# One decoder layer on one core: probabilities times values as unsplit fp32, two heads in two column groups

## What is computed

```python
probs = jax.nn.softmax(jnp.where(mask, q @ k.T * SCALE + bias, -jnp.inf), axis=-1)
y_head = probs @ v                                   # own
y_head = g0 * (p_cmp @ v_cmp) + g1 * (p_slc @ v_slc) + g2 * (p_win @ v_win)   # NSA, gates g
x = x + (sig(gA) * (y_A @ W_A) + sig(gB) * (y_B @ W_B)) @ W_o
x = x + (gelu(conv_a) * conv_b) @ W_down             # conv of rms_norm(x) @ W_up
x = x + sig(x @ W_pg) * (p @ W_pp)
```

## Time and profile before

| | us |
|---|---|
| median of 3 runs (lowest, highest) | 928.82 (927.83, 929.5) |
| the profiled execution | 928.06 |
| its span | 926.0 |
| TensorE busy | 888.6 (96%) |
| VectorE, ScalarE, GpSimd busy | 426.5, 411.1, 434.7 |
| attention steps, roughly | 88 to 410 |

### The profile page before, as it was taken

The page is one execution under the profiler, slowest core; times in us unless marked ns, Lnnn a source line. Parts: engine busy times, 40 slices in busy tenths (PEclk is TensorE's granted clock), DMA queues, the critical chain, the costliest instruction groups (busy, mean ns, idle before and its releaser), DMA issues.

```text
span 926.0 us, 13400 instructions
## 1 busy us (share of the span) xinstructions
PE 888.6 (96%) x4601; PEld 766.5 (83%) x4601; DVE 426.5 (46%) x961; ACT 411.1 (44%) x893; POOL 434.7 (47%) x557
## 2 busy tenths in 40 slices
PE   8999899998999799999999999999999999999998
PEld 8898798897899678787788788888888888888886
DVE  5445756866756545545412644444444440021124
ACT  5224554654746354644344454444444442232321
POOL 4841653554533433655363374444444445454350
PEclk9999999999999899999999999999999999999999
DMA  6835323333121034436543453333333333332213
GB/s 205 183 97 151 101 67 95 89 68 95 46 58 47 14 91 133 139 127 228 183 143 91 137 160 93 101 93 101 91 92 96 98 97 108 101 92 91 91 58 136
DMA packets 101365, 99.33 MB, mean 107 GB/s; under 512 B 15956, under 2 KB 76084, under 8 KB 101300
## 3 DMA queue, kind: packets, MB, share of 16 engines
q1 hardware_dynamic: 101247, 98.48, 36.4%
q10 hardware_dynamic: 53, 0.01, 0.0%
HBM read 87.58 MB, written 10.88 MB: 106 GB/s over the span
## 4 chain that ended last, share of the span: by engine, by line
PE 82%; DVE 7%; POOL 3%; ACT 3%; issue 3%; DMA 1%; SPq 0%; ACTq 0%; DVEq 0%; POOLq 0%
PE banks L1511 25%; PE banks L1513 24%; PE banks L1512 24%; PE banks L1662 2%; PE banks L1642 1%; PE banks L1641 1%; DVE plain_arena L1263 1%; PE banks L1571 1%; DVE split_arena L1282 1%; PE banks L1599 1%; ACT split_arena L1008 1%; DMA plain_arena<-gates 1%; DVE split_arena L1195 1%; DVE plain_arena L1296 1%; DMA plain_arena<-in_conv_w_dram 1%
## 5 line engine op out<-in xcount | busy, mean ns | idle before, releaser
L1511 PE MATMUL banks<-split_arena 128*128 128x512 f32 (+4 forms) x1228 | 464.5, 378 | 16.6 <-POOL split_arena L670 7.2
L1513 PE MATMUL banks<-split_arena 128*128 128x512 f32 (+4 forms) x1228 | 454.6, 370 | 0.0
L1512 PE MATMUL banks<-split_arena 128*128 128x512 f32 (+4 forms) x1228 | 454.3, 370 | 0.0
L694 POOL TENSOR_TENSOR split_arena<-plain_arena,split_arena 128x512 fp32r<-128x512 f32 x184 | 241.3, 1324 | 254.1 <-ACT split_arena L936 234.8
L1511 PEld LDWEIGHTS banks<-split_arena 128*128 128x128 f32 x1228 | 231.6, 189 | 56.1 <-POOL split_arena L670 8.6
L1513 PEld LDWEIGHTS banks<-split_arena 128*128 128x128 f32 x1228 | 231.6, 189 | 35.5
L1512 PEld LDWEIGHTS banks<-split_arena 128*128 128x128 f32 x1228 | 231.9, 189 | 32.0
L936 ACT ACTIVATE split_arena<-plain_arena 128x512 fp32r<-128x512 f32 x184 | 113.0, 628 | 192.5 <-PE banks L1513 178.8
L1469 DVE SCALAR_TENSOR_TENSOR plain_arena<-banks,plain_arena 128x511 f32<-128x511 f32 x44 | 32.7, 743 | 133.2 <-ACT plain_arena L1048 133.2
L895 ACT ACTIVATE plain_arena<-plain_arena 128x128 f32<-128x128 f32 (+1 forms) x96 | 54.0, 562 | 65.0 <-DVE plain_arena L1296 64.6
L709 POOL TENSOR_SCALAR plain_arena<-plain_arena 128x128 f32<-128x128 f32 (+1 forms) x64 | 40.7, 636 | 72.8 <-DVE plain_arena L1313 72.6
(11 more groups left out here) (170 smaller groups left out, 822.9 us busy)
## 6 DMA issues: line engine op xcount, KB each, us to landing
plain_arena<-in_w_up_dram SPq DMA_DIRECT2D x88, 256.0 KB, 3.1
plain_arena<-in_w_down_dram SPq DMA_DIRECT2D x44, 256.0 KB, 2.6
plain_arena<-in_w_in_dram SPq DMA_DIRECT2D x18, 512.0 KB, 4.5
plain_arena<-in_w_in_dram SPq DMA_DIRECT2D x32, 192.0 KB, 4.2
plain_arena<-in_x_dram SPq DMA_DIRECT2D x8, 512.0 KB, 5.4
gates<-plain_arena SPq DMA_DIRECT2D x16, 256.0 KB, 2.0
plain_arena<-skew SPq DMA_DIRECT2D x16, 256.0 KB, 4.1
plain_arena<-gates SPq DMA_DIRECT2D x16, 256.0 KB, 4.1
```

What stands on the lines that cost most here:

```text
L694: pool.tensor_tensor(W2l[:, c % RING, :], raw2[:, c % RING, :], W2h[:, c % RING, :].bitcast(F32), ALU.subtract).then_inc(w2_lo, 1)
L1511: nc.tensor.matmul(o, ah, bh, start=first, stop=False)
L1512: nc.tensor.matmul(o, ah, bl, start=False, stop=False)
L1513: return nc.tensor.matmul(o, al, bh, start=False, stop=last)
```

## The change

Probabilities and values are no longer split. Both are kept in plain fp32: `take_probs` (ScalarE) copies the turned probabilities once, `pt_low` is gone; `take_values` (GpSimd) copies the values once, `v_high` and `v_low` are gone, and so are the low part of the compressed values and its two operations. The values have no zero padding: a matmul takes 64 weight columns and writes 64 partitions, head 0 to partitions 0 to 63, head 1 to 64 to 127 of bank 6. The order of the steps in an NSA pair is changed to branches outside and heads inside, and the product is issued once for a branch (`due`), with key tiles outside and the two heads inside. The ring of probabilities has four units. `values_of` counts the blocks after which a unit's ring place is free. The arenas are laid out anew.

```diff
@@ attention_steps
-        for e in range(2):
-            for br in (["own"] if n < 4 else ["slc", "win"]):
+        for br in (["own"] if n < 4 else ["slc", "win"]):
+            for e in range(2):
                 for i in range(NT):
-                    steps.append(dict(n=n, e=e, br=br, i=i, u=u, last=(i == NT - 1), first=False, k=0))
+                    steps.append(dict(n=n, e=e, br=br, i=i, u=u, due=(e == 1 and i == NT - 1), first=False, k=0))
                 u += 1
@@ buffers
-        PTh = R[:, 16384:20480].rearrange("p (u j q) -> p u j q", u=2, j=NT)
-        PTl = R[:, 20480:24576].rearrange("p (u j q) -> p u j q", u=2, j=NT)
...
-        Vh = R[:, 30720:33792].rearrange("p (s t c) -> p s t c", s=4, t=NT)
-        Vl = R[:, 33792:36864].rearrange("p (s t c) -> p s t c", s=4, t=NT)
+        PT = AF[:, 0:8192].rearrange("p (u j q) -> p u j q", u=4, j=NT)
+        V = AF[:, 8192:10240].rearrange("p (s t c) -> p s t c", s=4, t=NT)
+        VC = AF[:, 10240:10496].rearrange("p (g c) -> p g c", g=2)
@@ gpsimd
-            def v_low(w):
...
+            def take_values(w):
                 n = w - 1
...
+                pool.wait_ge(qkv_done, 4 * w + 4)
+                if n >= 4:
+                    pool.wait_ge(pv_done, (n - 4) // 2 + 1)
+                pool.tensor_copy(V[:, vslot(n)], qkv[:, :, 256:384]).then_inc(v_done, 1)
@@ scalar
-            def v_high(w):
...
-            def pt_high(t):
+            def take_probs(t):
                 s = STEPS[t]
+                u, i = s["u"], s["i"]
                 act.wait_ge(turned, t + 1)
-                if s["u"] >= 2:
-                    act.wait_ge(pv_done, s["u"] - 1)
+                if u >= 4:
+                    act.wait_ge(pv_done, values_of[u - 4])
...
-            act.wait_ge(vc_lo, 1)
-            nc.scalar.activation(VCl[32:32 + NCMP, :, DH:2 * DH], VCl[0:NCMP, :, 0:DH].bitcast(F32), ACT.Copy).then_inc(vc_both, 1)
@@ vector
-            def pt_low(t):
...
@@ tensor, turn_probs
                 if t >= 2:
-                    pe.wait_ge(pt_lo, t - 1)
+                    pe.wait_ge(pt_done, t - 1)
@@ tensor, values
-                pe.wait_ge(pt_lo, t + 1)
-                opening = u == STEPS[first_t[n]]["u"]
+                pe.wait_ge(pt_done, t + 1)
+                opening = s["br"] in ("own", "slc")
...
-                c0 = 0 if e == 0 else DH
                 if s["br"] == "cmp":
-                    pe.wait_ge(vc_both, 1)
-                    g = (n - 4) // 2
-                    ins = three(PS[:, 6, :], VCh[:, g, :], VCl[:, g, :], PTh[:, u % 2, 0, :], PTl[:, u % 2, 0, :], False, closing)
+                    ins = nc.tensor.matmul(PS[:, 6, :], VC[:, (n - 4) // 2, :], PT[:, u % 4, 0, :], start=False, stop=closing)
                 else:
-                    vs = vslot(n, s["br"])
-
-                    for j in (reversed(range(NT)) if closing else range(NT)):
-                        q = slice(P * j, S)
-                        ins = three(PS[:, 6, q], Vh[:, vs, j, c0:c0 + P], Vl[:, vs, j, c0:c0 + P], PTh[:, u % 2, j, q], PTl[:, u % 2, j, q],
-                                    opening and j == 0, closing and j == 0)
+                    for j in range(NT):
+                        for h in range(2):
+                            c0 = DH * (h if n < 4 else s["br"] == "win")
+                            ins = nc.tensor.matmul(PS[DH * h:DH * (h + 1), 6, P * j:S], V[:, vslot(n), j, c0:c0 + DH], PT[:, (u - 1 + h) % 4, j, P * j:S],
+                                                   start=opening and j == 0, stop=closing and j == NT - 1)
                 ins.then_inc(pv_done, 1)
@@ tensor, main loop
-                if t >= VLAG and STEPS[t - VLAG]["last"]:
+                if t >= VLAG and STEPS[t - VLAG]["due"]:
                     values(t - VLAG)
```

More of the change, by code:

```diff
@@ L10 @@
+import itertools
 from contextlib import ExitStack
@@ L55, in attention_steps @@
     for n in range(NPAIR):
-        for e in range(2):
-            for br in (["own"] if n < 4 else ["slc", "win"]):
+        for br in (["own"] if n < 4 else ["slc", "win"]):
+            for e in range(2):
                 for i in range(NT):
-                    steps.append(dict(n=n, e=e, br=br, i=i, u=u, last=(i == NT - 1), first=False, k=0))
+                    steps.append(dict(n=n, e=e, br=br, i=i, u=u, due=(e == 1 and i == NT - 1), first=False, k=0))
                 u += 1
         if n >= 4:
-            steps.append(dict(n=n, e=0, br="cmp", i=0, u=u, last=True, first=False, k=0))
+            steps.append(dict(n=n, e=0, br="cmp", i=0, u=u, due=True, first=False, k=0))
             u += 1
@@ L78, in layer @@
     NSTEP = [last_t[n] - first_t[n] + 1 for n in range(NPAIR)]
-    unit_last_t = {s["u"]: t for t, s in enumerate(STEPS) if s["last"]}
+    values_count = list(itertools.accumulate(s["due"] for s in STEPS))
+    values_of = {s["u"]: values_count[t] + (not s["due"]) for t, s in enumerate(STEPS)}
     def ucols(w):
@@ L200, in sem, with r3 @@
             return ctx.enter_context(nc.semaphore(n))
-        R = ctx.enter_context(nc.sbuf_tensor("split_arena", [P, 38912], F32R))
+        R = ctx.enter_context(nc.sbuf_tensor("split_arena", [P, 16384], F32R))
         F = ctx.enter_context(nc.sbuf_tensor("plain_arena", [P, 14280], F32))
+        with ExitStack() as attention:
+            AF = attention.enter_context(nc.sbuf_tensor("attention_plain", [P, 10496], F32))
+            AR = attention.enter_context(nc.sbuf_tensor("attention_split", [P, 7296], F32R))
+        L = ctx.enter_context(nc.sbuf_tensor("late_arena", [P, 22528], F32R))
         PS = ctx.enter_context(nc.psum_tensor("banks", [P, 8, 512], F32))
-        def r3(o, a, b):
-            return R[:, o:o + a * b].rearrange("p (a b) -> p a b", a=a)
+        def r3(o, a, b, arena=R):
+            return arena[:, o:o + a * b].rearrange("p (a b) -> p a b", a=a)
         def f3(o, a, b):
@@ L658, in _ @@
                                pattern=[[-1, P]], channel_multiplier=1).then_inc(pool_const, 1)
-            for t_ in (Vh, Vl):
-                pool.memset(t_[:, :, :, DH:2 * DH].bitcast(F32), 0.0).then_inc(pool_const, 1)
-            for t_ in (VCh, VCl, KCh, KCl):
+            pool.memset(VC, 0.0).then_inc(pool_const, 1)
+            for t_ in (KCh, KCl):
                 pool.memset(t_.bitcast(F32), 0.0).then_inc(pool_const, 1)
@@ L762, in _ @@
             split_unit(2, range(KT))
-            v_low(1)
+            take_values(1)
             split_gate(2)
@@ L997, in _ @@
                 if LAG <= t:
-                    pt_high(t - LAG)
+                    take_probs(t - LAG)
                 if t - 1 in TURN:
@@ L1012, in _ @@
                     w_high(*SPLIT[t])
-                if t in VALUES and VALUES[t] != 6:
-                    v_high(VALUES[t])
                 if t in EARLY:
@@ L1800, in _ @@
                 if T + c < T + VLAG:
-                    if STEPS[T + c - VLAG]["last"]:
+                    if STEPS[T + c - VLAG]["due"]:
                         values(T + c - VLAG)
```

99 lines of the change are left out of this document (26 added, 73 removed).

## The result

| | before | after |
|---|---|---|
| median of 3 runs, us (lowest, highest) | 928.82 (927.83, 929.5) | 921.95 (921.45, 923.7) |
| profiled execution, us (span) | 928.06 (926.0) | 921.95 (919.8) |
| mean granted clock over the span | 0.996 | 0.984 |

What follows compares the result with a forecast made beforehand. The attention stage was taken as bound by TensorE's own work, with short stalls behind GpSimd and VectorE. 928.8 - 11.8 (TensorE work) - 8 (stalls) = 909 us, range 901 to 933.

Steps and rivals of the forecast that it cites:

- The passes: Value product: each unsplit fp32 matmul is two instructions of two passes each, 0.44 us per instruction at 512 columns.
- The overlap: Value product: both heads' matmuls run at the same time in nine slots, 2.8 us a branch against 3.94; chance 0.58.
- The rival of groups one after the other: Value product: the two heads run in series without a drain, +8.4 us on TensorE, 927 to 929 us; chance 0.17.
- The drain: Array drain around the branch blocks, twice a branch: 1.2 us in all taken, a third of the upper bound 3.9.
- TensorE sum: TensorE's work: branches -12.5 us with the drain share, compressed steps +0.7, together -11.8 us.
- The stalls: TensorE's waits in the attention and the slow clock behind them: 8 us of 15 gained, with 3 and 13 as ends.
- (a): Longest TensorE stall, at 302 us behind GpSimd's scaling: 4.67 us idle and 3.2 us of slow clock, 7.9 together.
- (b): Step 5 of pairs 1 to 3: three TensorE waits of 1.65 to 1.72 us for GpSimd splits; most of 5 us goes.
- What is late next is nothing by more than 0.5: At the longest stall, near 302 us: once it is relieved, nothing else is late by more than 0.5 us.
- The clock rival: Half-array blocks lower the granted clock to 1.2 GHz behind a third of the 12 branches: +16 us, 925; chance 0.03.
- After 412 us there is no change of work: Everything behind the attention stage: no work changes, and the forecast sum has no term for it.
- The wait at 85.83: TensorE's 0.58 us wait, put behind ScalarE's wait for the low part of the compressed values: it goes.

Runs made afterwards that it cites:

- e_heads_outside: The changed kernel with the value product's two inner loops exchanged, four key tiles of head 0, then four of head 1: 937.32 us, 1.007 of the kernel before.
- e_per_head: The changed kernel with the value product issued per head again, each in its own steps (8, 12, 16, 3): 932.2 us, 1.002 of the kernel before.
- e_gate_first: The changed kernel with ScalarE serving the merge gate's hand-over first in its step and VectorE's low part moved earlier: 913.16 us, 0.982 of the kernel before.
- e_fill: The changed kernel with ten unused fp32 matmuls ahead of pairs 6 and 7 and the first weight chunk: 916.44 us, 0.985 of the kernel before.
- e_before_gate: The kernel before the change, with only the merge gate's hand-over served earlier by ScalarE and VectorE: 931.97 us, 1.002 of the kernel before.
- e_best: The changed kernel with `plain_arena` placed last and, in the NSA pairs alone, the merge gate's hand-over served earlier: 905.2 us, 0.974 of the kernel before.
- r_after: The changed kernel run again unedited, as base for the follow-up runs: 923.49 us, 0.992 of the kernel before.

## Why the prediction was right or wrong

- **Direction and range**: faster, and 921.95 lies between 901 and 933. The size was wrong: 7 us instead of 20.
- **The passes**: right. Two passes per instruction; behind 512 columns the next instruction of one head starts 0.43 us later, against 0.44.
- **The overlap**: right, and under-sized. The nine slots assumed that instructions start in order. In the trace TensorE takes the other head's instruction ahead of the waiting second half, so there are eight slots: 2.30 us and not 2.8, worth 6 us more than forecast. The rival of groups one after the other falls with e_heads_outside. The page "TensorE: Matmul & The Clock Gate", Part 3, of the Trainium skill has matmuls in distinct column groups run at the same time: the trace agrees, also for fp32 with 512 columns (2.30 us for two heads, 2.29 for one).
- **The drain**: 1.2 us were put in, up to 3.9 in the range. The block as a whole, from its first start to that of the next work, is 2.30 us, while 1280 columns in two instructions of two passes at 2.4 GHz are 2.13 us and eight starts at 12 ns are 0.1. That leaves 0.1 us inside the block. Behind it the next work loses 0.11 us (the second matmul there starts 0.28 us behind the first, at 384 columns, and not 0.17), and in front of it at most 0.1 (its first start is 0.20 us behind the last transpose's, where two transposes are 0.11 to 0.13 apart). Together it is 0.2 to 0.3 us a block, about the 0.2 that the forecast had for the change of form and the drain. The page "TensorEngine Tiling (Array Packing)", Key Properties, of the Trainium skill has a change of mode drain TensorE; if these 0.2 to 0.3 us are that drain, which no run here tells, it costs no more.
- **TensorE sum**: -17.7 (-19.7, +0.7 and +1.3) in place of -11.8.
- **The stalls: this is the step that failed.** Removing (a) and (b) was right, both in place and in size (4.67 to 0.49 us, 1.72 to 0.42). The sentence "What is late next is nothing by more than 0.5" was wrong, since it looked only for what stood behind GpSimd in the same place. Moving the values was costed where they arrive ("+0.8 us there") and, where they left, counted only as a chance to catch up. They had been the cover of the gate hand-over, and what waits in steps 9 and 0 once they are gone was not asked. Instead of 8 us gained the waits gave 0.7, and the clock took 6.8: 14 us short of the forecast. e_per_head closes the waits again, e_gate_first gains 9 us by shortening the hand-over, e_fill 6 by filling the waits, and in the kernel before the same reorder gains nothing (e_before_gate).
- **The clock rival** (0.03) was right that the clock would fall and wrong in its cause. The half array does it no harm: e_heads_outside keeps 0.984, e_per_head with twice the narrow blocks has 0.998. It falls in and behind waits of TensorE of some 3 us, and e_fill takes that away by filling three of them.
- **"After 412 us there is no change of work"**: true of the work, not of its time. This is a second step that failed, a term put at nothing: the new arenas cost 4.8 us there, 3.5 of them in the down projection.
- **The number**: 909 + 14.1 (waits and clock) + 4.8 (layout) - 5.9 (TensorE's work) is 922. That 921.95 lies in the range owes something to luck: the overlap gained more than forecast and paid for part of the two steps that failed. With both largely mended, e_best comes to 905.2 us.
- **The wait at 85.83**: it was to go with the low part of the compressed values. It stands unchanged, 0.58 us at 85.30. Its row named ScalarE's projection copy (L831) all along, and in ScalarE's timeline that copy waits for TensorE's own projection (L1513, 1.33 us), not for the low part.
- **VectorE** lost 44 us of busy time instead of 49.

## What to carry to other kernels

When a block of matmuls is moved or merged, look for two places, not one: where it goes, and what it had been hiding where it stood. List TensorE's short waits behind every chain of other engines that runs between two of its tasks, and add the block's length to each that loses it; here a wait that grew by 1.9 us, to 3.25, cost 2 us more, since the granted clock was low behind it. And compare the start-to-start time of one unchanged stage before and after: it shows at once what a new layout of SBUF costs.

## What the runs showed of the hardware

- Two fp32 matmuls with 64 weight columns each, on different halves of the output partitions, run entirely side by side at 512 columns, also when each is two instructions: first starts 7 ns apart, and eight such matmuls, four a head, take 2.30 us, where one head's four take 2.29.
- TensorE starts a matmul for the other half of the array ahead of up to three earlier ones of the first half, and not of more (e_heads_outside: 1.56 us into the block). The full overlap was seen only with the two streams alternating in the program.
- Around waits of 3.2 to 3.3 us the granted clock was at 1.2 GHz for 6.8 us three times of four and for 3.4 once in the changed kernel. The three long stretches began while TensorE still waited, so that 2.1 to 2.4 us each were lost, and 1.7 by the short one; 2.3 us of matmuls without use in such a wait kept the clock at 2.4 GHz. The same wait is not always followed alike: 3.17 us at pair 4 had no slow stretch in e_fill and r_after, and 1.75 us at 106.05 had one here and none in the kernel before.
- Behind a block of matmuls with 64 weight columns the second of the next 128-column matmuls starts 0.28 us behind the first at 384 columns, and not 0.17.
- 512-column matmuls start 233 ns apart when the streamed operand's arena starts 32 bytes past a multiple of 64, 229 with 8 words more, and 227 where it lay before.
